# 72 instead of 48 tiles of an expert up-projection in the stage beside the choice of the experts, their results held in 48 places used in turn

## The chip, the core and the metric

One core of one Trainium2 chip runs the whole program. The metric is the device time of one execution in microseconds; the median of several executions is compared. The engines are named as in the profile: PE (matrix products, PEld its weight loads), DVE (vector), ACT (activations), POOL and SP (both used here mainly to issue transfers).

## The reference, cut to what matters

The model is two blocks over 256 tokens of width 2048. The change lies in the last layer of the second block, a mixture of 16384 tiny experts, each one row of `u_tab` and one row of `v_tab`:

```python
def peer(h, w_q, sub_keys, u_tab, v_tab):
    q = (h @ w_q).reshape(bsz, length, 8 heads, 2, 64)
    s = einsum("blhsk,hsnk->blhsn", q, sub_keys)        # scores against 2 x 128 keys
    s1, i1 = top_k(s[..., 0, :], 16); s2, i2 = top_k(s[..., 1, :], 16)
    cand_s = s1[..., :, None] + s2[..., None, :]         # 256 pairs per head
    top_s, pos = top_k(cand_s, 16)                       # 16 experts per head and token
    idx, g = take_along_axis(cand_i, pos), softmax(top_s)
    act = gelu(einsum("td,tkd->tk", x, u_tab[idx]))
    return einsum("tk,tkd->td", g * act, v_tab[idx])
```

## The kernel before, in words

The kernel does not gather rows. It computes gelu(x u) for all 16384 experts, multiplies by a gate that is zero where an expert was not chosen, and multiplies with all of `v_tab`. The 16384 experts are 128 tiles of 128; one tile is 128 experts by 256 tokens. The tensor `gates` holds 128 places of 256 columns.

All linear layers run through `linear_stage` (line 655). A tile's weights are four quarters of 512 columns. Each quarter goes through three engines: SP loads pairs of quarters into `ring` (`stream`), ACT rounds a quarter into `weights_hi` (`make_hi`, L200), DVE subtracts to get `weights_lo` (`make_lo`, L207), and PE multiplies both parts (L846, 32 matmuls a tile). `weights_hi` and `weights_lo` have four slots each, so one tile's quarters lie ready ahead of PE. After a tile ACT copies half of its sum out of PSUM (L760), DVE adds the other half (L816), and ACT applies gelu (L2456). All engines work in the order in which their instructions are written; semaphores tie them together: `core.multiplied` (a quarter is used up), `core.rounded`, `core.split`, `core.moved`, `core.summed`, `core.shaped` (gelu is done).

The order of the stages around the change, in `second_block` (line 2404):

1. `experts_first`: the first 48 tiles (EARLY_TILES) of the up-projection. Beside it runs the choice of the experts, `ExpertChoice` (line 2136). Its scores are on PE before the first and after the first tile; the searches (MAX8, FIND_INDEX8 and MATCH_REPLACE8 over 32 rows of 128 columns and 16 rows of 256 columns, each search in two rounds) and 14 large steps over 2048 columns are on DVE. `after_split` is called behind each split of a quarter and runs as many steps of the generator `vector` as are due: the planned nanoseconds of all steps (COLUMNS, 112260) are spread evenly over the quarters from the 9th (FIRST = 8) up to `self.quarters` = 4 x (tiles - 6). What is left runs after the stage's last tile. The arrays of the choice lie in `gates` from place EARLY_TILES to 115, the keys and queries in the last 12.
2. Gelu of early tile n goes to place n of `gates`. `ExpertChoice.issue` on POOL stores four tiles at a time to DRAM (`saved`, L2164) and waits for all stores at the end.
3. `gates_stage` (line 2322) writes the gates of all 128 tiles over the whole of `gates`.
4. `experts`: the remaining up-projection tiles, each multiplied into its gate (L2474), and then 128 tiles of down-projection. Beside the up-projection, `Returned` (line 2298) loads the stored tiles in pairs into two slots of `acts_back` (L2313, on POOL) and multiplies each into its gate on DVE (L2319, in `after_tile`). They are spread evenly over all but the last four tiles of the layer.

A layer with something beside it is written out tile by tile on PE, ACT and DVE; others run in loops.

Of the kernel before, what the change touches and what calls it, by code (L numbers as in the profile page):

```python
# [58 lines left out]
PEER_HEADS = 8  # L59
KEYS = 128  # L60
TOPK = 16
EARLY_TILES = 48
TWO_PI = 6.283185
MAGIC = 12582912.0

# [348 lines left out]
class Beside:  # L414
# [4 lines left out]
    def issue(self, pool):  # L419
        pass  # L420
# [1532 lines left out]
def glu_stage(core, y, parts, next_w):  # L1953

    with core.nc.Block() as block:
        @block.scalar
        def _(act):
            act.activation(y, y, ACT.Gelu_apprx_tanh)

    def gate(dve, n, slots):  # L1960
        dve.tensor_tensor(y[:, n, :], y[:, n, :], slots[0], ALU.mult)

    linear_stage(core, "glu", [
        Layer("w_glu", HT, [parts], shape=lambda act, n, slots: act.activation(slots[0], slots[0], ACT.Sigmoid),
              finish=gate, quarters=2, source=y)], next_w)
# [170 lines left out]
class ExpertChoice(Beside):  # L2136
# [23 lines left out]

    def issue(self, pool):
        for g in range(self.tiles // 4):
            pool.wait_ge(self.core.shaped, self.shaped + 4 * g + 4)
            pool.dma_start(self.saved[g], self.acts[:, 4 * g:4 * g + 4, :]).then_inc(self.done["saved"], 16)  # L2164
        pool.wait_ge(self.done["saved"], 16 * (self.tiles // 4))

    def scores(self, pe, t):
        for a in range(2):
# [225 lines left out]
def onto_stream(core, last=True):  # L2394

    def finish(dve, n, slots):
        ins = dve.tensor_tensor(core.x[:, n, :], core.x[:, n, :], slots[0], ALU.add)
        if last:
            core.dve.step(dve, ins)
            add_squares(core, dve, n, slots[0])  # L2400
    return finish


def second_block(core, out):


    nc = core.nc

    class S5:
        pass  # L2410

    with ExitStack() as mixers:
        sb = lambda name, shape, dt=F32: mixers.enter_context(nc.sbuf_tensor(name, shape, dt))
        proj, conv = sb("proj", [P, 3 * HT, T]), sb("conv", [P, HT, T])
        scans = ExitStack()
        sb2 = lambda name, shape: scans.enter_context(nc.sbuf_tensor(name, shape, F32))
        s5 = S5()
        s5.b, s5.c, s5.r = sb2("s5_b", [P, HT, 2, 2, 64]), sb2("s5_cc", [P, 3, PAIRS, 32]), sb2("s5_r", [P, PAIRS])
        with ExitStack() as projections:
            sb3 = lambda name, shape, dt=F32: projections.enter_context(nc.sbuf_tensor(name, shape, dt))  # L2420
            parts, h = sb3("in2_parts", [P, KD, 2, T], F32R), sb3("h_in2", [P, KD, T])
            rows = lambda part: (lambda n: proj[:, n + part * HT, :])
            linear_stage(core, "in2", [
                Layer("w_in_2", HT, [parts], into=rows(0), source=h, norm=Norm(core.x, core.prm["norm_mix"])),
                Layer("w_in_2", HT, [parts], first=2 * HT,
                      shape=lambda act, n, slots: act.activation(slots[0], slots[0], ACT.Sigmoid),
                      finish=lambda dve, n, slots: dve.tensor_copy(proj[:, n + HT, :], slots[0])),
                Layer("w_in_2", HT, [parts], first=4 * HT, into=rows(2)),
            ], ("w_glu", 0), beside=MixerSetup(core, s5, sb3))
        with scans:  # L2430
            local_mixers_stage(core, s5, proj, conv)
        y = proj[:, 2 * HT:, :]
        with nc.sbuf_tensor("glu_parts", [P, HT, 2, T], F32R) as parts:
            glu_stage(core, y, parts, ("w_out_2", 0))
        mem_parts = sb("mem_parts", [P, KD, 2, T], F32R)
        with ExitStack() as out2:
            sb2 = lambda name, shape, dt=F32: out2.enter_context(nc.sbuf_tensor(name, shape, dt))
            parts, h = sb2("out2_parts", [P, KD, 2, T], F32R), sb2("h_out2", [P, KD, T])
            mem, mem_squares = sb2("mem", [P, KD, T]), sb2("mem_squares", [P, KD, T])
            mem_sum, mem_std = sb2("mem_sum", [P, 1, T]), sb2("mem_std", [P, T])  # L2440
            group_norm_stage(core, conv[:], y, h)
            linear_stage(core, "mix2_out", [Layer("w_out_2", KD, [parts], finish=onto_stream(core), source=h, squares=True, steps=3)],
                         ("w_k", 0), loads=[(mem[:], "mem")], squares_of=(mem_squares[:], mem_sum[:]),
                         beside=NormBeside(core, mem, mem_sum[:, 0, :], core.prm["mem_norm"], mem_std[:], mem,
                                           mem_parts, at=5, squared=core.loaded_squared))
        q, k, v = proj[:, 0:KD, :], sb("k", [P, KD, T]), sb("v", [P, TT, 4, BANK])
        parts, h, std = sb("att_parts", [P, KD, 2, T], F32R), sb("h_att", [P, KD, T]), sb("att_std", [P, T])
        linear_stage(core, "mem_k", [Layer("w_k", KD, [mem_parts], into=lambda n: k[:, n, :])], ("w_q", 0),
                     beside=NormBeside(core, core.x, core.squares, core.prm["norm_mem"], std[:], h, parts))
        linear_stage(core, "mem_q", [Layer("w_q", KD, [parts], into=lambda n: q[:, n, :])], ("w_v", 0))  # L2450
        values_stage(core, mem_parts, v, ("w_o", 0))
        attention_stage(core, q, k, v, parts, h)
        linear_stage(core, "mem_out", [Layer("w_o", KD, [parts], finish=onto_stream(core), squares=True, steps=3)], ("w_peer_q", 0))
    with nc.sbuf_tensor("expert_parts", [P, KD, 2, T], F32R) as parts, nc.sbuf_tensor("gates", [P, KEYS, T], F32) as gates:
        saved = nc.dram_tensor("saved_acts", (EARLY_TILES // 4, P, 4, T), F32, kind="Internal").ap()
        gelu = lambda act, out, slots: act.activation(out, slots[0], ACT.Gelu_apprx_tanh)  # L2456
        with nc.sbuf_tensor("turned", [P, 3, T], F32) as turned:
            q = gates[:, KEYS - 8:KEYS, :]
            keys = gates[:, KEYS - 12:KEYS - 8, :].rearrange("p a (h n) -> p (a h) n", n=KEYS)
            linear_stage(core, "peer_q", [Layer("w_peer_q", PEER_HEADS, [parts], into=lambda n: q[:, n, :],  # L2460
                                                source=gates[:, 0:KD, :],
                                                norm=Norm(core.x, core.prm["norm_ffn"], squares=core.squares))],
                         ("w_u", 0), loads=[(keys, "peer_keys")])
            choice = ExpertChoice(core, q, keys, turned, gates[:, EARLY_TILES:KEYS - 12, :], gates[:, 0:EARLY_TILES, :], saved,
                                  EARLY_TILES, 6)
            linear_stage(core, "experts_first", [
                Layer("w_u", EARLY_TILES, [parts], shape=lambda act, n, slots: gelu(act, gates[:, n, :], slots)),
            ], ("w_u", 2 * EARLY_TILES), begin_next=False, beside=choice)
            gates_stage(core, turned, gates)
        with nc.sbuf_tensor("acts_back", [P, 4, T], F32) as back:  # L2470

            def gate_experts(dve, n, slots):
                at = n + EARLY_TILES
                dve.tensor_tensor(gates[:, at, :], gates[:, at, :], slots[0], ALU.mult)  # L2474

            up = Layer("w_u", KEYS - EARLY_TILES, [parts], finish=gate_experts, first=2 * EARLY_TILES,
                       shape=lambda act, n, slots: gelu(act, slots[0], slots))
            chunks = KEYS // KD
            down = [Layer("w_v_tab", KD, [parts], finish=onto_stream(core, c == chunks - 1), first=c * 2 * KD,
                          source=gates[:, c * KD:(c + 1) * KD, :], squares=c == chunks - 1,  # L2480
                          steps=3 if c == chunks - 1 else 0) for c in range(chunks)]
            linear_stage(core, "experts", [up, *down], None,
                         beside=Returned(core, back, saved, gates, EARLY_TILES, KEYS - EARLY_TILES - 4))
    rms_stage(core, "norm_last", core.x, core.x, KD, core.prm["final2"], squares=core.squares, store=out)
# [33 lines left out]
def two_block_kernel(nc, dram, out):  # L2518
    with ExitStack() as ctx:
        core = Core(nc, ctx, dram)  # L2520
        first_block(core)
        second_block(core, out)
# [127 lines left out]
```

## Time and profile before

| | us |
|---|---|
| median of 3 runs | 4280.64 (4276.46 to 4289.01) |
| profiled execution | 4285.37 |
| its span, first to last instruction | 4283.6 |
| PE busy / DVE busy / ACT busy | 3877.2 / 2815.2 / 2064.3 |
| stage beside the choice, 2nd to 47th gelu | 282.63 |
| up-projection after it, 2nd to 79th gelu | 427.87 |

The page gives each engine's busy time as a share of the span; a high share says that an engine is nearly always at work, and not in which stage it is late. The trace can be asked for stretches of time, for waits and for single instructions; times in it count from the span's start.

### The profile page before, as it was taken

How to read it: one execution, taken by the hardware profiler on the slowest of the kernel's cores; microseconds unless marked ns; L12 is line 12 of the kernel's file. 1: busy time of each engine (PE TensorE's matmuls, PEld its weight loads, DVE VectorE, ACT ScalarE, POOL GpSimd, SP SyncE). 2: the span in 40 equal slices, each digit the busy share in tenths (PEclk: the TensorE clock that was granted, in tenths of full speed). 3: DMA queues.
4: the chain of work that ended last, by engine and by line, in shares of the span. 5: the costliest groups of instructions: out<-in, count | busy, mean ns of one | idle time of the engine just before them, and what ended most of it. 6: DMA issues, size and time to landing. Idle time of an engine off the chain costs nothing. (4 is left out here: it accounts for less than half of the span.)

```text
span 4283.6 us, 66352 instructions
## 1 busy us (share of the span) xinstructions
PE 3877.2 (91%) x22156; PEld 3171.7 (74%) x22156; DVE 2815.2 (66%) x5280; ACT 2064.3 (48%) x3828; POOL 203.6 (5%) x242
## 2 busy tenths in 40 slices
PE   6699968778999999887699998998799999999998
PEld 0467744567888888774588877877688888888887
DVE  0553435777888667679686557687966666666667
ACT  0442330235666555455455434444955555555554
POOL 3011100000000000103100000000000000000000
PEclk9899979988999999998899999999999999999999
DMA  9686720034766666441255535555066665666665
GB/s 340 230 302 248 264 92 0 1 106 152 214 214 211 190 188 189 153 150 60 99 177 185 180 110 167 168 184 184 5 200 205 203 203 186 188 189 187 190 189 159
DMA packets 199380, 735.10 MB, mean 172 GB/s; under 512 B 22903, under 2 KB 22936, under 8 KB 197400
## 3 DMA queue, kind: packets, MB, share of 16 engines
q1 hardware_dynamic: 173992, 639.97, 47.6%
q0 software_dynamic: 25200, 92.64, 5.9%
q8 instruction: 116, 1.90, 0.2%
q14 instruction: 72, 0.59, 0.1%
HBM read 715.74 MB, written 16.78 MB: 171 GB/s over the span
## 5 line engine op out<-in xcount | busy, mean ns | idle before, releaser
L207 DVE TENSOR_TENSOR weights_lo<-ring,weights_hi 128x512 fp32r<-128x512 f32 x2240 | 1528.0, 695 | 978.1 <-ACT weights_hi L200 962.5
L200 ACT ACTIVATE weights_hi<-ring 128x512 fp32r<-128x512 f32 x2240 | 1396.4, 630 | 1373.9 <-PE ps L846 1308.4
L846 PE MATMUL ps<-expert_parts,weights_hi 128*128 128x512 f32 x4224 | 1466.9, 395 | 34.3 <-DVE weights_lo L207 26.8
L846 PE MATMUL ps<-expert_parts,weights_lo 128*128 128x256 f32 x4224 | 1142.6, 281 | 0.0
L846 PEld LDWEIGHTS ps<-expert_parts,weights_hi 128*128 128x128 f32 x4224 | 780.7, 189 | 205.2 <-issue 36.4
L846 PEld LDWEIGHTS ps<-expert_parts,weights_lo 128*128 128x128 f32 x4224 | 797.7, 189 | 20.4
L846 PE MATMUL ps<-mlp_parts,weights_hi 128*128 128x512 f32 x1024 | 354.0, 394 | 16.7 <-PEq L604 15.8
L846 PE MATMUL ps<-hidden,weights_hi 128*128 128x512 f32 x1024 | 351.5, 392 | 0.6 <-DVE weights_lo L207 0.6
L846 PE MATMUL ps<-mlp_parts,weights_lo 128*128 128x256 f32 x1024 | 277.4, 281 | 0.0
L846 PE MATMUL ps<-h_parts,weights_hi 128*128 128x512 f32 x704 | 266.1, 406 | 11.8 <-DVE weights_lo L207 11.8
L846 PE MATMUL ps<-hidden,weights_lo 128*128 128x256 f32 x1024 | 276.3, 280 | 0.0
L846 PEld LDWEIGHTS ps<-mlp_parts,weights_hi 128*128 128x128 f32 x1024 | 189.1, 189 | 55.5 <-issue 17.7
L846 PEld LDWEIGHTS ps<-hidden,weights_hi 128*128 128x128 f32 x1024 | 187.8, 188 | 38.4 <-DVE weights_lo L207 0.9
L846 PEld LDWEIGHTS ps<-mlp_parts,weights_lo 128*128 128x128 f32 x1024 | 193.8, 189 | 5.3
L377 PE MATMUL ps<-ada_ring,silu_c 128*32 128x512 f32 x768 | 148.9, 625 | 53.0 <-DMA ada_ring<-in_w_ada 52.9
L846 PEld LDWEIGHTS ps<-hidden,weights_lo 128*128 128x128 f32 x1024 | 192.5, 188 | 5.4
L846 PE MATMUL ps<-h_parts,weights_lo 128*128 128x256 f32 x704 | 193.2, 283 | 0.0
L846 PEld LDWEIGHTS ps<-h_parts,weights_hi 128*128 128x128 f32 x704 | 133.3, 190 | 75.1 <-issue 45.0
L846 PE MATMUL ps<-att_parts,weights_hi 128*128 128x512 f32 x512 | 176.1, 393 | 3.9 <-PEq L677 2.4
L846 PE MATMUL ps<-in_parts,weights_hi 128*128 128x512 f32 x384 | 136.7, 401 | 15.8 <-DVE weights_lo L207 8.5
L846 PEld LDWEIGHTS ps<-h_parts,weights_lo 128*128 128x128 f32 x704 | 133.5, 190 | 8.8
L846 PE MATMUL ps<-att_parts,weights_lo 128*128 128x256 f32 x512 | 138.1, 280 | 0.0
(460 smaller groups left out, 4972.7 us busy)
## 6 DMA issues: line engine op xcount, KB each, us to landing
ring<-in_w_mlp SPq DMA_DIRECT2D x256, 512.0 KB, 3.7
ring<-in_w_u SPq DMA_DIRECT2D x256, 512.0 KB, 4.1
ring<-in_w_v_tab SPq DMA_DIRECT2D x256, 512.0 KB, 3.7
ada_ring<-in_w_ada POOLq DMA_DIRECT2D x124, 512.0 KB, 6.5
ring<-in_w_mix SPq DMA_DIRECT2D x88, 512.0 KB, 5.6
ada_ring<-in_w_ada SPq DMA_DIRECT2D x68, 512.0 KB, 5.2
ring<-in_w_out SPq DMA_DIRECT2D x64, 512.0 KB, 3.7
ring<-in_w_in SPq DMA_DIRECT2D x48, 512.0 KB, 4.0
```

What stands on the lines that cost most here:

```text
L200: act.activation(core.hi[:, g % SLOTS], core.ring[:, slot, at:at + QUARTER], ACT.Copy).then_inc(core.rounded, 1)
L207: dve.tensor_tensor(core.lo[:, g % SLOTS], core.ring[:, slot, at:at + QUARTER], core.hi[:, g % SLOTS].bitcast(F32), ALU.subtract).then_inc ...
L377: mm = pe.matmul(self.core.ps[32 * j:32 * j + 32, self.bank(part), :], self.cond[:, k, :], self.ring[:, slot, (j % 2) * BANK:(j % 2 + 1) * ...
L846: mm = pe.matmul(out, part[:, g % SLOTS, k, :], moving, start=at == 0 and part is core.hi, stop=last and part is core.hi)
```

## The change

The number of early tiles and the number of places that hold their results become two constants. 72 tiles run beside the choice; tile n goes to place n mod 48. Before gelu of a tile from the 49th on, ACT waits until the store of the group that had this place has landed. POOL now waits after each store for it to land, so that the counter tells which stores are done. The arrays of the choice stay in places 48 to 115. The planned steps of the choice are spread over 4 x 66 - 8 = 256 quarters where it was 4 x 42 - 8 = 160. The later layer has 56 tiles where it had 80, and `Returned` brings back 72 tiles beside 52 of them where it brought 48 beside 76.

```diff
-EARLY_TILES = 48
+EARLY_TILES, EARLY_SLOTS = 72, 48
...
     def issue(self, pool):
         for g in range(self.tiles // 4):
+            at = 4 * g % EARLY_SLOTS
             pool.wait_ge(self.core.shaped, self.shaped + 4 * g + 4)
-            pool.dma_start(self.saved[g], self.acts[:, 4 * g:4 * g + 4, :]).then_inc(self.done["saved"], 16)
-        pool.wait_ge(self.done["saved"], 16 * (self.tiles // 4))
+            pool.dma_start(self.saved[g], self.acts[:, at:at + 4, :]).then_inc(self.done["saved"], 16)
+            pool.wait_ge(self.done["saved"], 16 * (g + 1))
+
+    def act_slot(self, act, n):
+        if n >= EARLY_SLOTS:
+            act.wait_ge(self.done["saved"], 16 * ((n - EARLY_SLOTS) // 4 + 1))
+        return self.acts[:, n % EARLY_SLOTS, :]
...
-            choice = ExpertChoice(core, q, keys, turned, gates[:, EARLY_TILES:KEYS - 12, :], gates[:, 0:EARLY_TILES, :], saved,
+            choice = ExpertChoice(core, q, keys, turned, gates[:, EARLY_SLOTS:KEYS - 12, :], gates[:, 0:EARLY_SLOTS, :], saved,
                                   EARLY_TILES, 6)
             linear_stage(core, "experts_first", [
-                Layer("w_u", EARLY_TILES, [parts], shape=lambda act, n, slots: gelu(act, gates[:, n, :], slots)),
+                Layer("w_u", EARLY_TILES, [parts], shape=lambda act, n, slots: gelu(act, choice.act_slot(act, n), slots)),
```

## Rows read from the trace of the kernel before

**Rows 1.** The page: busy time by engine, and the costliest groups of ACT and DVE.
```profile
PE 3877.2 (91%) x22156; PEld 3171.7 (74%) x22156; DVE 2815.2 (66%) x5280; ACT 2064.3 (48%) x3828; POOL 203.6 (5%) x242
...
L207 DVE TENSOR_TENSOR weights_lo<-ring,weights_hi 128x512 fp32r<-128x512 f32 x2240 | 1528.0, 695 | 978.1 <-ACT weights_hi L200 962.5
L200 ACT ACTIVATE weights_hi<-ring 128x512 fp32r<-128x512 f32 x2240 | 1396.4, 630 | 1373.9 <-PE ps L846 1308.4
```

**Rows 2.** Two stretches: busy time of each engine, beside and after the choice.
```profile
core 0: us, PE busy (x) PEld busy (x) DVE busy (x) ACT busy (x) POOL busy (x), PEclk, DMA share, GB/s
2710.19:2992.82 282.63, 259.19 (x1439) 219.44 (x1438) 228.53 (x619) 127.95 (x270) 5.96 (x11) 1.00 0.59 188
3122.23:3550.10 427.87, 427.87 (x2465) 376.28 (x2465) 279.12 (x510) 239.59 (x463) 11.84 (x22) 1.00 0.66 203
```

**Rows 3.** Timeline of ACT (start, duration): gelu of four tiles.
```profile
2710.19 0.42 ACT L2456 ACTIVATE gates<-experts_first_sums 128x256 f32<-128x256 f32 x1 [1.21 <-DVE experts_first_sums L816]
...
2992.82 0.42 ACT L2456 ACTIVATE gates<-experts_first_sums 128x256 f32<-128x256 f32 x1 [0.82 <-DVE experts_first_sums L816]
...
3122.23 0.42 ACT L2456 ACTIVATE experts_sums<-experts_sums 128x256 f32<-128x256 f32 x1 [0.82 <-DVE experts_sums L816]
...
3550.10 0.42 ACT L2456 ACTIVATE experts_sums<-experts_sums 128x256 f32<-128x256 f32 x1 [0.82 <-DVE experts_sums L816]
```

**Rows 4.** Waits, 2710 to 2993 us: total, times, longest.
```profile
PE ps L846 <- DVE weights_lo L207: 23.4, 36, 1.3
```

**Rows 5.** Timeline of DVE over one tile beside the choice.
```profile
2716.93 0.69 DVE L207 TENSOR_TENSOR weights_lo<-ring,weights_hi 128x512 fp32r<-128x512 f32 x1 [1.01 <-ACT weights_hi L200]
2717.54 0.48 DVE L2238 MAX8 gates<-gates 128x8 f32<-128x128 f32 x2
2717.94 0.68 DVE L207 TENSOR_TENSOR weights_lo<-ring,weights_hi 128x512 fp32r<-128x512 f32 x1
...
2721.29 0.40 DVE L816 TENSOR_TENSOR experts_first_sums<-experts_first_sums,ps 128x256 f32<-128x256 f32 x1
2722.70 0.69 DVE L207 TENSOR_TENSOR weights_lo<-ring,weights_hi 128x512 fp32r<-128x512 f32 x1 [1.01 <-ACT weights_hi L200]
```

**Rows 6.** Timeline of DVE: searches of 128 and of 256 columns.
```profile
2724.44 0.09 DVE L2243 MATCH_VALUE_LOAD gates<-gates 128x8 f32 x1
...
2725.23 0.67 DVE L207 TENSOR_TENSOR weights_lo<-ring,weights_hi 128x512 fp32r<-128x512 f32 x1
...
2882.37 0.09 DVE L2243 MATCH_VALUE_LOAD gates<-gates 128x8 f32 x1
...
2883.17 0.67 DVE L207 TENSOR_TENSOR weights_lo<-ring,weights_hi 128x512 fp32r<-128x512 f32 x1
```

**Rows 7.** Timeline of DVE: one of the 14 large steps.
```profile
2902.47 2.29 DVE L2285 TENSOR_TENSOR gates<-gates 128x2048 f32<-128x2048 f32 x1
2904.79 1.29 DVE L207 TENSOR_TENSOR weights_lo<-ring,weights_hi 128x512 fp32r<-128x512 f32 x2
```

**Rows 8.** Timeline of DVE over one tile of the later stage.
```profile
3177.35 0.41 DVE L816 TENSOR_TENSOR experts_sums<-experts_sums,ps 128x256 f32<-128x256 f32 x1
3178.25 0.42 DVE L2474 TENSOR_TENSOR gates<-gates,experts_sums 128x256 f32<-128x256 f32 x1 [0.48 <-ACT experts_sums L2456]
3178.59 0.42 DVE L2319 TENSOR_TENSOR gates<-gates,acts_back 128x256 f32<-128x256 f32 x1
3178.93 1.29 DVE L207 TENSOR_TENSOR weights_lo<-ring,weights_hi 128x512 fp32r<-128x512 f32 x2
3180.97 0.69 DVE L207 TENSOR_TENSOR weights_lo<-ring,weights_hi 128x512 fp32r<-128x512 f32 x1 [0.76 <-ACT weights_hi L200]
```

**Rows 9.** DMA issues: KB each, median us from issue to landing.
```profile
saved_acts<-gates POOLq DMA_DIRECT2D x12, 512.0 KB, 3.8
acts_back<-saved_acts POOLq DMA_DIRECT2D x24, 256.0 KB, 3.9
...
context<-in_ctx POOLq DMA_DIRECT2D x1, 2048.0 KB, 17.2
```

## The prediction

> **What bounds the kernel now.** I read the page's totals first: PE is busy for 91% of the span, DVE for 66% [rows 1]. So the question is only where PE stands still, and whether the change touches such a place. The change touches the two stages of the expert up-projection, so I read the table of stretches for both [rows 2]. In the stage beside the choice (2710 to 2993 us) PE is busy 259.2 of 282.6 us; in the stage after it (3122 to 3550 us) it is busy all of the 427.9 us. Both have PE at a granted clock of 1.00, and both do the same matmuls per tile.
>
> The price of one tile comes from the starts of gelu, one per tile [rows 3]. In the later stage 77 intervals take 3550.10 - 3122.23 = 427.87 us, 5.557 us a tile: PE's own pace. In the stage beside the choice 45 intervals take 2992.82 - 2710.19 = 282.63 us, 6.281 us a tile. At PE's pace they would be 250.06 us. So 32.6 us are lost there. The list of waits says to whom: PE waited 23.4 us in 36 pieces for DVE's low parts of the weights [rows 4], about the 23.4 us by which PE's busy time falls short. The rest of the 32.6 is not waited for by a busy-time count (ends of matmuls are modelled), so I take the tile pace, not the busy time.
>
> DVE is busy only 228.5 of 282.6 us there [rows 2], 81%, and still it is the bound. The timeline of one tile shows why [rows 5]. After DVE's sum (L816, start 2721.29) the next split (L207) starts at 2722.70, 1.41 us later, of which 1.01 us is idle: ACT has to do gelu of this tile (0.42 us, [rows 3]) and then round the next quarter of weights (0.63 us, [rows 1]) before DVE has anything to split. Four splits then follow, each 0.60 us after the other's start (0.61 from 2716.93 to 2717.54). So a DVE that lags needs 1.41 + 4 x 0.60 = 3.81 us a tile beside the steps of the choice. Check: this tile holds ten MAX8, two in 0.40 us; 3.81 + 10 x 0.20 = 5.81 against 5.77 measured.
>
> How much is the choice? DVE's busy time less its linear work is 228.53 - 45 x (4 x 0.60 + 0.41) = 102.1 us, and some 7 MAX8 (1.4 us) come before that stretch: 103.5 us. The code deals it out over 4 x 42 - 8 = 160 quarters, 40 tiles: 2.59 us a tile, and 3.81 + 2.59 = 6.40 us. Over 40 tiles that is 0.84 too much each, 34 us, against the 32.6 found. The model holds.
>
> **The change part by part.**
>
> *The choice over 72 tiles.* The share per quarter falls from 112260/160 = 702 to 112260/256 = 439 of the code's planned nanoseconds. The same 103.5 us lie on 64 tiles, 1.62 us each: 3.81 + 1.62 = 5.43 us, below PE's 5.557. DVE no longer bounds on the average, and the 32.6 us go. This is the only gain.
>
> Average isn't all. Where the real step is dearer than planned, a phase could still be over PE's pace. Searches: a FIND_INDEX8 of 256 columns with its load costs 0.40 us (two from 2882.37 to 2883.17), planned 0.416; one of 128 columns 0.26 us (three from 2724.44 to 2725.23), planned 0.288 [rows 6]. At 1754 planned ns a tile these are 4.2 x 0.40 = 1.69 and 6.1 x 0.26 = 1.60 us: 5.50 and 5.41, below 5.557. The 14 large steps cost 2.32 us (2902.47 to 2904.79) [rows 7], planned 2.2, and come every fifth quarter: four tiles with one and one without take 5 x 3.81 + 4 x 2.32 = 28.3 us against 27.8 of PE. Over their 17 tiles that is 2 us too much. Does the buffer hide it? A slot of weights is used again three quarters (4.17 us) after PE has freed it, and rounding and splitting take 0.63 + 0.70 us [rows 1], so DVE may lag some 2.8 us before PE stops. Bounds: 0 (the lag never reaches 2.8), and no buffer at all, where each large step stalls its tile by 3.81 + 2.32 - 5.56 = 0.57 us, 14 of them 8 us, and each second tile of the 46 in the searches (five steps instead of four) by 0.26 us, 6 us: 14 us. I take 2 us, near the lower end, since a lag of 0.6 a tile is far below 2.8.
>
> *24 tiles move.* They leave the later stage and enter the first: 24 x 5.557 us out, 24 x 5.557 in, if both keep PE's pace. Zero. The written-out instruction streams cover 48 + 80 = 128 tiles before and 72 + 56 after.
>
> *Their return.* 24 more products on DVE, now 72 beside 52 tiles, one or two a tile. In a tile with one, DVE goes from the sum (3177.35) to the product with the gate (3178.25), to the returned product (3178.59), to the split (3178.93), and has 0.76 us idle later [rows 8]. Its loop is 1.58 + 4 x 0.60 = 3.98 us, with two returned products 0.34 more, 4.32 us. Both fit in 5.557. PE hides it. If that cover were gone, it would be 24 x 0.34 = 8 us. Each product waits on DVE for a load from DRAM; behind it stand all splits. Loads take 3.9 us from issue to landing [rows 9]. One is issued when its slot is free, three products ahead of its first use, at least two tiles or 11.1 us. 7 us of slack: zero.
>
> *Stores.* Six more on POOL, and POOL now waits for each to land: 3.8 us [rows 9] in a period of four tiles, 22 us. Zero. Behind these waits only the next store is queued. The last store of the stage is issued and awaited as before. ACT gets 24 waits before its gelu for tiles 48 to 71; each is for a store some 44 tiles, 240 us, old. Not shown in the trace: between 0 and the 0.05 us from the sum's end (3177.35 + 0.41) to gelu's start, 3177.80 by the same spacing, that a due wait costs, 24 times, 1 us, off PE's path while DVE keeps up. I take 0. DMA carries 3.1 MB more each way; its share of the later stage, 0.66 [rows 2], would rise to about 0.72, with no wait of PE on DMA now: zero.
>
> Scores, the tail of the choice, the gates stage and the down-projection stay as they are.
>
> **Sum.** Profiled execution 4285.4 (span 4283.6 and 1.8 around it) - 32.6 + 2 = 4254.8 us. The median of the runs shown is 4.7 us lower, 4280.6; on that scale 4250 us.
>
> **The rivals.**
>
> *A, no buffer.* The steps' lumps reach PE: 14 us stay. 4285.4 - 32.6 + 14 - 4.7 = 4262 us. For it: tiles with one large step took 6.1 us and more; against it: those tiles were already lagging.
>
> *B, DVE still bounds, nearly no gain.* Reckon DVE by whole durations instead of starts: 0.41 + 1.01 + 4 x 0.69 + the choice. MAX8 pairs shown as 0.48 us instead of 0.40 make the choice 103.5 x 1.2 = 124 us, 1.94 a tile: 6.12 us. 64 tiles x 0.56 = 36 us would stay, no gain: 4281 us. Against it: split follows split at 0.60 us though it lasts 0.69, and the same reckoning for the tile of rows 5 gives 4.18 + 2.4 = 6.6 us, where 5.77 were measured. The Trainium skill (VectorE: DVE Perf Modes, section "The DRAIN you can't avoid") has the rule that speaks for B: the next vector operation does not start before the pipe of the one before is empty. By that rule the sum would be B's 4281 us instead of 4250; this case's trace, with its 0.60 against 0.69, disagrees.
>
> *C, slower: the loads of the returned tiles.* 36 pairs now come back within 52 tiles, one pair in 8.0 us, through two slots. A slot's turn is the load plus the 4 us between the two uses of a pair, so the period of a pair is (L + 4)/2 once L passes 12 us. At L = 13.8 it is 8.9 us and the 34 later pairs eat the gain; from there the kernel is slower. At 17.2 us, the slowest load of that queue shown (of 2 MB, [rows 9]), the period is 10.6 us: 34 x 2.6 = 88 us, 4250 + 88 = 4338 us. For it: the DMAs of that queue run beside 200 GB/s of weights; against it: they do so now, and take 3.9 us.
>
> **How the numbers follow.** Forecast 0.77, A 0.12, B 0.07, C 0.04. A measurement of this kernel can tell about 0.3%, 13 us, from no change: faster means below 4268. Forecast and A are faster: 0.89. B is the same: 0.07. C is slower: 0.04. The range starts at the forecast without the 2 us and with 6 us for the scatter of runs (4276 to 4289 shown): 4242. It ends past A with as much scatter: 4267.
>
> **What would show it.** In the stretch beside the choice gelu starts should be 5.56 us apart from start to end, PE's waits for L207 near zero, DVE's 1.01 us idle after the sum split into shorter ones behind each split. The stage should last about 72 x 5.557 + 13 us. The later stage should keep 5.56 us a tile with one and two L2319 beside it. A large-step phase with intervals of 6.1 us means A; intervals near 6.1 us throughout mean B; DVE waits for acts_back mean C. I am wrong if the two stages together save less than 18 us.

## The result, and the profile after

The changed kernel takes 4250.5 us (median, 4248.0 to 4262.6), the kernel before 4282.0 us in the same comparison: ratio 0.9930 (0.9916 to 0.9944), 31.4 us by the medians. The forecast was 4250 us. That the medians meet to within 1 us is luck: the four runs of the changed kernel spread over 14.6 us.

The page of the profile first. It hardly moved from [rows 1]; PE is busy for 91% of the span in both kernels:

```profile
PE 3872.2 (91%) x22156; PEld 3171.5 (74%) x22156; DVE 2807.8 (66%) x5280; ACT 2067.4 (49%) x3828; POOL 213.5 (5%) x260
```

Next the stages that were touched: from the second to the next to last gelu beside the choice, as in [rows 2], and from the first to the 54th gelu after it (columns as there).

```profile
2717.92:3103.97 386.05, 384.40 (x2207) 336.63 (x2206) 300.98 (x742) 206.38 (x414) 9.14 (x17) 1.00 0.67 211
3227.15:3521.66 294.51, 294.51 (x1697) 258.88 (x1697) 201.69 (x390) 164.88 (x319) 18.28 (x34) 1.00 0.73 220
```

PE is now busy 384.4 of 386.1 us beside the choice. The timeline of ACT gives the pace:

```profile
2717.92 0.42 ACT L2462 ACTIVATE gates<-experts_first_sums 128x256 f32<-128x256 f32 x1 [1.20 <-DVE experts_first_sums L816]
...
3103.97 0.42 ACT L2462 ACTIVATE gates<-experts_first_sums 128x256 f32<-128x256 f32 x1 [0.82 <-DVE experts_first_sums L816]
...
3227.15 0.42 ACT L2462 ACTIVATE experts_sums<-experts_sums 128x256 f32<-128x256 f32 x1 [0.82 <-DVE experts_sums L816]
...
3521.66 0.42 ACT L2462 ACTIVATE experts_sums<-experts_sums 128x256 f32<-128x256 f32 x1 [0.82 <-DVE experts_sums L816]
```

69 intervals take 386.05 us, 5.595 us a tile against 6.281 before [rows 3]. At 5.557 they would take 383.4, so 2.6 us are lost where 32.6 were. The later stage has 294.51/53 = 5.557 us a tile, as before. The waits of the first stretch (total, times, longest):

```profile
DVE weights_lo L207 <- ACT weights_hi L200: 82.4, 96, 1.0
ACT weights_hi L200 <- PE ps L846: 79.9, 119, 0.8
...
PE ps L846 <- DVE weights_lo L207: 1.6, 4, 0.5
```

PE waited 1.6 us for DVE, where it had waited 23.4 [rows 4]. ACT, in turn, waited 79.9 us for PE to free a slot of weights; before it was 13.0 us. One tile of DVE early in the choice, to be held against [rows 5]:

```profile
2718.89 0.69 DVE L207 TENSOR_TENSOR weights_lo<-ring,weights_hi 128x512 fp32r<-128x512 f32 x1 [1.00 <-ACT weights_hi L200]
2719.49 0.29 DVE L2244 MAX8 gates<-gates 128x8 f32<-128x128 f32 x1
2719.70 0.68 DVE L207 TENSOR_TENSOR weights_lo<-ring,weights_hi 128x512 fp32r<-128x512 f32 x1
2720.29 0.48 DVE L2244 MAX8 gates<-gates 128x8 f32<-128x128 f32 x2
2720.71 0.69 DVE L207 TENSOR_TENSOR weights_lo<-ring,weights_hi 128x512 fp32r<-128x512 f32 x1
2721.32 0.28 DVE L2244 MAX8 gates<-gates 128x8 f32<-128x128 f32 x1
2722.03 0.69 DVE L207 TENSOR_TENSOR weights_lo<-ring,weights_hi 128x512 fp32r<-128x512 f32 x1 [0.43 <-ACT weights_hi L200]
2722.64 0.48 DVE L2244 MAX8 gates<-gates 128x8 f32<-128x128 f32 x2
2723.04 0.40 DVE L816 TENSOR_TENSOR experts_first_sums<-experts_first_sums,ps 128x256 f32<-128x256 f32 x1
2724.45 0.69 DVE L207 TENSOR_TENSOR weights_lo<-ring,weights_hi 128x512 fp32r<-128x512 f32 x1 [1.01 <-ACT weights_hi L200]
```

Six MAX8 stand where ten stood. The 1.01 us behind the sum is still there, but before the fourth split DVE has a new idle stretch of 0.43 us: it has caught up with PE, and the chain waits for a slot. The prediction had said that the 1.01 us would split into shorter idle times behind each split; they stay, and shorter ones come beside them.

The profiled execution of the changed kernel is the slowest of its four, 4262.6 us (span 4260.7). Its extra time lies ahead of the change: the first score matmul (L2171 before, L2177 after) starts at 2692.65 us, before it started at 2684.90. So traces are best compared from there to the end of the span: 4283.6 - 2684.90 = 1598.7 us before, 4260.7 - 2692.65 = 1568.0 us after, 30.7 us less. The sum had said 32.6 - 2 = 30.6. Of the 30.7 us, 30.0 are the stage's own (32.6 - 2.6).

### The profile page after: what moved, and what is told of

Read it like the earlier page. It is cut to its first block and busy times, and to the rows that moved or that the text cites. A ratio compares the mean times of both kernels' runs of the same rounds, so it can differ in the third digit from the quotient of the medians.

```text
span 4260.7 us, 66415 instructions
## 1 busy us (share of the span) xinstructions
PE 3872.2 (91%) x22156; PEld 3171.5 (74%) x22156; DVE 2807.8 (66%) x5280; ACT 2067.4 (49%) x3828; POOL 213.5 (5%) x260
## 5 line engine op out<-in xcount | busy, mean ns | idle before, releaser
L846 PE MATMUL ps<-mlp_parts,weights_hi 128*128 128x512 f32 x1024 | 354.2, 394 | 16.7 <-PEq L604 15.8
```

The source lines that it names most:

```text
L846: mm = pe.matmul(out, part[:, g % SLOTS, k, :], moving, start=at == 0 and part is core.hi, stop=last and part is core.hi)
```

## The experiments

My theory: beside the choice DVE runs in a loop of 3.81 us a tile (sum, ACT's gelu and rounding, four splits) plus its share of the choice's 103.5 us. It binds while this is above PE's 5.557 us. The rivals: B (DVE is bound by its own instructions, counted in whole durations), C (the returned tiles), a gain from the small edits, and a gain that grows with each tile moved. In the table "from the scores" is the span's end less the start of the first score matmul in the run's trace. Each ratio is to the kernel before as it ran in the same comparison; its medians there were 4284.4 us (e1 to e4), 4280.0 us (e5 to e7) and 4285.9 us (e8 to e10).

| run | median us | ratio to before | from the scores, us | less than before |
|---|---|---|---|---|
| before | 4282.0 | | 1598.7 | |
| changed | 4250.5 | 0.9930 (0.9916 to 0.9944) | 1568.0 | 30.7 |
| e1_edits_48 | 4283.0 | 0.9997 (0.9988 to 1.0007) | 1598.7 | 0.0 |
| e2_tiles_60 | 4257.7 | 0.9936 (0.9919 to 0.9953) | 1579.8 | 18.9 |
| e3_late_gelu_48 | 4255.7 | 0.9933 (0.9916 to 0.9949) | 1569.0 | 29.7 |
| e4_late_gelu_72 | 4249.2 | 0.9915 (0.9896 to 0.9933) | 1564.5 | 34.2 |
| e5_tiles_96 | 4265.8 | 0.9962 (0.9950 to 0.9975) | 1582.0 | 16.7 |
| e6_back_26 | 4250.1 (one run) | | 1566.5 | 32.2 |
| e7_back_12 | 4302.0 (one run) | | 1611.4 | -12.7 |
| e8_places_96 | 4251.3 | 0.9925 (0.9909 to 0.9942) | 1565.7 | 33.0 |
| e9_after_again | 4253.5 | 0.9926 (0.9914 to 0.9938) | 1565.9 | 32.8 |
| e10_late_72_again | 4249.5 | 0.9914 (0.9901 to 0.9926) | 1564.6 | 34.1 |

The changed kernel and e9 are the same kernel; their 1568.0 and 1565.9 us show how far this count scatters from trace to trace, some 2 us. Most of it arises between the last gelu beside the choice and the first of the later stage: 117.64 us in the first trace, 115.29 in e9 (first row below: changed; second: e9). The instructions there are the same. At the start of the later stage the granted clock stood at 0.50 for some 7 us in the first trace and at 1.00 in e9 (third and fourth row: 16 matmuls against 29 in the same 6.7 us):

```profile
3109.51:3227.15 117.64, 86.95 (x561) 73.72 (x562) 104.48 (x332) 103.46 (x205) 1.62 (x3) 0.93 0.07 22
3100.47:3215.76 115.29, 83.83 (x561) 71.23 (x562) 104.50 (x332) 103.37 (x204) 1.62 (x3) 0.97 0.07 22
3215.60:3222.30 6.70, 5.08 (x16) 4.33 (x17) 3.46 (x6) 2.82 (x5) 1.08 (x2) 0.50 0.63 213
3206.50:3213.20 6.70, 5.00 (x29) 4.44 (x30) 4.16 (x7) 3.95 (x7) 1.09 (x2) 1.00 0.65 191
```

The traces of before, e1 and e2 have such a stretch too, e6, e7 and e9 have none, the others one of half the length. So up to 3 us of the last column can come from it, and the loss against PE's pace within a stage is the sharper count.

**The small edits alone.**

```diff
-EARLY_TILES, EARLY_SLOTS = 72, 48
+EARLY_TILES, EARLY_SLOTS = 48, 48
```

> The changed kernel with 48 early tiles: POOL waits after each store and the other edits stay, the number of tiles is that of before. Theory (DVE's loop of 3.81 us a tile plus the choice's share is the bound, only the spreading over more tiles helps): same as before, ratio 1.000, 6.28 us a tile beside the choice. Rival (POOL's waits after each store, or another of the small edits, gives part of the gain): faster than before by up to 30 us.

Measured: 0.9997. Its 45 intervals lost 32.5 us, before it was 32.6. POOL's waits after each store neither cost nor gain. ACT's new wait does not occur with 48 tiles, so this run says nothing of it.

**60 early tiles** (EARLY_TILES = 60).

> 60 early tiles. Theory: the choice's 103.5 us lie on 52 tiles, 1.99 us each; 3.81 + 1.99 = 5.80 us a tile, 0.24 above PE's 5.557, so 52 x 0.24 = 13 us stay lost of 32.6: about 20 us faster than before, ratio 0.9954, and some 5.8 us between gelu starts while the choice runs. Rival (each moved tile brings the same, 30 us / 24 = 1.25 us): 12 tiles bring 15 us, ratio 0.9965.

The medians give 26.7 us, with an interval of about 20 to 35: the theory's 20 lies at its edge, the rival's 15 outside. The trace settles it better. From the second to the next to last gelu there are 57 intervals:

```profile
2703.66 0.42 ACT L2462 ACTIVATE gates<-experts_first_sums 128x256 f32<-128x256 f32 x1 [1.21 <-DVE experts_first_sums L816]
...
3034.24 0.42 ACT L2462 ACTIVATE gates<-experts_first_sums 128x256 f32<-128x256 f32 x1 [0.82 <-DVE experts_first_sums L816]
```

They take 330.58 us, 13.8 us above 57 x 5.557 (the theory said 13). The count from the scores gives 18.9 us less than before. Half of the added tiles brings some 60% of the gain (18.9 of 30.7): the curve bends as a loop does that comes down to PE's pace.

**Gelu behind the next rounding, 48 tiles.** EARLY_TILES is 48. ACT's order alone is changed: gelu of a tile is put aside and runs behind the next quarter that ACT rounds. DVE has the same work at the same places.

```diff
+        layer.late = isinstance(beside, ExpertChoice)
...
+                if make is make_hi and layer.late:
+                    def make_layer(core, act, g, i, per, base):
+                        make_hi(core, act, g, i, per, base)
+                        while waiting:
+                            waiting.pop(0)()
...
                     if layer.shape is not None:
-                        act.wait_ge(core.summed, i * layer.unroll + (layer.N + s + 3))
-                        layer.shape(act, n, slots(layer, n, s)).then_inc(core.shaped, 1)
+                        def late():
+                            act.wait_ge(core.summed, i * layer.unroll + (layer.N + s + 3))
+                            layer.shape(act, n, slots(layer, n, s)).then_inc(core.shaped, 1)
+                        if layer.late and n < layer.tiles - 1:
+                            waiting.append(late)
+                        else:
+                            while waiting:
+                                waiting.pop(0)()
+                            late()
```

> 48 early tiles, but ACT rounds the first quarter of the next weights before it does gelu of the tile. DVE has the same work. Theory (the 1.01 us in which DVE waits for ACT's gelu and rounding is part of the loop): the wait falls to about 0.25 us (rounding 0.63 us begins with DVE's sum of 0.41 us), the loop to 3.05 us, with the choice 2.59 it is 5.64 us a tile; some 3 us and lumps of the large steps stay, 3 to 10 us in all: 23 to 29 us faster than before, ratio 0.993 to 0.995. Rival B (DVE is bound by its own work alone, counted in whole durations, 6 us and more a tile): no change, ratio 1.000.

Measured: 0.9933; 29.7 us less from the scores, 0.7 us above the 23 to 29 us expected, which is less than the scatter. The 44 intervals from the second gelu on lost 3.4 us. The timeline of DVE in this run, a tile with ten MAX8 as in [rows 5]:

```profile
2764.55 0.40 DVE L829 TENSOR_TENSOR experts_first_sums<-experts_first_sums,ps 128x256 f32<-128x256 f32 x1
2764.87 0.69 DVE L207 TENSOR_TENSOR weights_lo<-ring,weights_hi 128x512 fp32r<-128x512 f32 x1
2765.47 0.48 DVE L2257 MAX8 gates<-gates 128x8 f32<-128x128 f32 x2
2766.13 0.69 DVE L207 TENSOR_TENSOR weights_lo<-ring,weights_hi 128x512 fp32r<-128x512 f32 x1 [0.18 <-ACT weights_hi L200]
```

The split follows the sum at once and the 1.01 us is gone. The waits of 0.2 us elsewhere are PE's pace: ACT, for which DVE waits there, itself waited 78.8 us for PE in this stretch, where it had been 13.0. So nearly the whole gain can be had without moving a tile. This rules out rival B: with the same DVE instructions the loss fell from 32.6 to 3.4 us. And it says what had been the bound: a chain from DVE over ACT and back, and not DVE's work by itself.

**Both together.**

> 72 early tiles and gelu behind the next rounding. Theory: the loop is 3.05 + 1.62 = 4.67 us, 0.9 us below PE's pace, and even a tile with a large step needs 3.05 + 2.32 = 5.37 us, so nothing of the 2.6 us is left: 5.557 us between gelu starts throughout, ratio to before 0.992, to the changed kernel not distinguishable. Rival (the 2.6 us come from where the large steps stand among the quarters): they stay.

PE waited for DVE not once between 2710 and 3088 us in this trace; the 68 intervals from the second gelu on lost nothing (-0.4 us). The rival (the lumps stay) falls. I had said 5.557 us between gelu starts throughout; that was wrong in form, since gelu itself is late (up to 7.4 us apart) behind the large steps, without PE noticing. From the scores it is 34.2 us less than before.

**96 early tiles** (EARLY_TILES = 96).

> 96 early tiles, 96 returned beside 28. Theory: beside the choice 3.81 + 103.5/88 = 4.99 us, below PE's 5.557, with large steps every seventh quarter; 0 to 1 us stays lost in that stage, some 2 us less than with 72. More moved tiles bring nothing else: ratio to before about 0.992 if the returns stay hidden. Rival C (the loads of the returned tiles bind): three or four products stand behind one another in a tile, DVE's loop is 3.64 + 3.43 x 0.34 = 4.8 us plus a wait for the load of up to 1 us: up to 7 us lost over 28 tiles, ratio 0.994. Rival (the gain grows with the tiles moved, 1.25 us each): 60 us, ratio 0.986.

Measured: 0.9962, so 16.3 us by the ratio and 16.7 from the scores, half of what I expected. The stage beside the choice did nearly as the theory says (93 intervals lost 1.5 us, 0 to 1 expected). The loss is in the later stage: 30 intervals of gelu from 3356.96 us take 182.95 us, 16.2 above PE's pace, where I had allowed 7. The waits from 3356.96 to 3534.36 us show rival C at work:

```profile
DVE gates L2325 <- DMA acts_back<-saved_acts: 17.2, 10, 3.4
```

One such wait in DVE's timeline, the issue of its load on POOL, and PE's and ACT's timelines around it:

```profile
3463.97 1.11 DVE L2325 TENSOR_TENSOR gates<-gates,acts_back 128x256 f32<-128x256 f32 x3
3468.52 0.42 DVE L2325 TENSOR_TENSOR gates<-gates,acts_back 128x256 f32<-128x256 f32 x1 [3.44 <-DMA acts_back<-saved_acts]
3468.86 2.49 DVE L207 TENSOR_TENSOR weights_lo<-ring,weights_hi 128x512 fp32r<-128x512 f32 x4
```
```profile
3464.69 1.21 POOL L2319 DMA_DIRECT2D acts_back<-saved_acts  x2 [4.46 <-DVE gates L2325]
```
```profile
3469.69 0.47 PE L846 MATMUL ps<-expert_parts,weights_hi 128*128 128x512 f32 x1 [2.72 <-DVE weights_lo L207]
...
3471.16 0.63 PE L846 MATMUL ps<-expert_parts,weights_hi 128*128 128x512 f32 x1
```
```profile
3463.17 0.42 ACT L2462 ACTIVATE experts_sums<-experts_sums 128x256 f32<-128x256 f32 x1 [0.82 <-DVE experts_sums L816]
...
3471.71 0.42 ACT L2462 ACTIVATE experts_sums<-experts_sums 128x256 f32<-128x256 f32 x1 [3.81 <-DVE experts_sums L816]
...
3478.82 0.42 ACT L2462 ACTIVATE experts_sums<-experts_sums 128x256 f32<-128x256 f32 x1 [0.82 <-DVE experts_sums L816]
```

A slot holds a pair and is loaded again only when both tiles are used. The products beside one tile form a batch, of three or four here. Where a batch of four starts with the second tile of a pair, its last tile belongs to the pair after the next, whose load starts only when the batch's first product has freed the slot. Here that product starts at 3463.97, the load at 3464.69, and it lands at 3468.5: DVE waits nearly a whole load (3.7 us in the median). Four of the batches meet the pairs in this way. I had counted an average; the pairs make it a matter of how batches and pairs meet.

**The returns packed closer, 72 tiles.** The last argument of `Returned`, 52 in the changed kernel, becomes 26 and 12.

> The changed kernel with its 72 tiles returned beside 26 up tiles instead of 52: 2.8 products a tile. Theory: DVE's loop is 3.64 + 2.8 x 0.34 = 4.6 us, a pair is due every 4.0 us, and its load (4.5 us with 2 slots) allows one about every 3.3 us: gelu starts stay 5.56 us apart. Rival C: they widen.

> 72 tiles returned beside 12 up tiles, six products a tile with two slots of two: the third pair of each tile can be loaded only after the first is used, so DVE waits about 3.8 us a tile; its loop is 3.64 + 6 x 0.34 + 3.8 = 9.5 us against 5.557, 12 tiles lose about 47 us, less 3 us for the weights laid ready. That is rival C made true: a wait for acts_back on DVE and gelu starts 9 to 10 us apart. If loads did not hold DVE, they would stay 5.7 us apart.

e6: 5.56 us a tile but for one of 6.32 us; DVE waited for loads twice, 2.2 us in all. As expected. e7: the first 13 intervals are 8.4 to 9.5 us long. Its one run takes 51.9 us more than that of e6. From the scores it is 44.9 us more than e6 and 43.4 more than the changed kernel (1611.4 against 1566.5 and 1568.0), where 44 were expected. The wait is the one named:

```profile
DVE gates L2325 <- DMA acts_back<-saved_acts: 40.3, 12, 3.8
...
PE ps L846 <- DVE weights_lo L207: 29.4, 12, 3.7
```

The granted clock was 0.87 in the mean over these 13 intervals (its column is the third from the end), for which the 44 us had no term; how much of the 43.4 us is the clock's isn't separated:

```profile
3221.02:3338.80 117.78, 88.42 (x417) 74.25 (x417) 66.80 (x150) 40.98 (x79) 18.29 (x34) 0.87 0.58 192
```

So rival C is real, and the change lies well clear of it at 1.4 products a tile.

**96 tiles, five places of one tile.** `acts_back` has five places of one tile instead of two of a pair, and a load brings one tile.

```diff
-        for m in range(0, self.tiles, 2):
-            slot = m // 2 % 2
-            if m >= 4:
-                pool.wait_ge(self.used, m - 2)
-            pool.dma_start(self.back[:, 2 * slot:2 * slot + 2, :], self.saved[m // 4, :, m % 4:m % 4 + 2, :]).then_inc(
-                self.landed[slot], 16)
+        for m in range(self.tiles):
+            if m >= 5:
+                pool.wait_ge(self.used, m - 4)
+            pool.dma_start(self.back[:, m % 5, :], self.saved[m // 4, :, m % 4, :]).then_inc(self.landed[m % 5], 16)
...
-            dve.wait_ge(self.landed[m // 2 % 2], 16 * (m // 4 + 1))
+            dve.wait_ge(self.landed[m % 5], 16 * (m // 5 + 1))
```

> 96 early tiles, returned one by one into five places instead of in pairs into two slots; three or four products a tile as in the run with 96 tiles and pairs, which lost 16 us there against PE's pace. Theory: a place is free as soon as its one tile is used, four of five lie ready at each batch, and the next four have 5.56 - 1.4 = 4.2 us and the fifth place to land: DVE waits little, 0 to 4 us stay of the 16 and no wait of 3 us. Ratio to before 0.992 to 0.993. Rival (the 16 us are the cost of more products on DVE, or of DMA traffic, whatever the slots): the 16 us stay, ratio 0.996.

Measured: 0.9925; gelu starts in the later stage:

```profile
3338.14 0.42 ACT L2460 ACTIVATE experts_sums<-experts_sums 128x256 f32<-128x256 f32 x1 [0.82 <-DVE experts_sums L816]
...
3504.84 0.42 ACT L2460 ACTIVATE experts_sums<-experts_sums 128x256 f32<-128x256 f32 x1 [0.82 <-DVE experts_sums L816]
```

30 intervals, 166.70 us, 5.557 each: all of the 16 us is back, with as many products and as much traffic. The slots were the cause. The run changes two things of them, one tile a load and room for a fifth tile, and no run tells which of the two does it. And 96 tiles bring no more than 72 (0.9925 against 0.9930 and 0.9926): the gain doesn't grow with the tiles once the loop is below PE's pace.

**The two best, side by side.**

> The changed kernel again, on the same chip as the next, to compare the two: ratio to before 0.993.

> 72 early tiles and gelu behind the next rounding, beside the changed kernel on the same chip. Theory: 2.6 us (0.06%) less than it, from the stage beside the choice; the medians lie 0 to 5 us apart. Rival: no difference at all, since the lag was hidden.

0.9926 (0.9914 to 0.9938) and 0.9914 (0.9901 to 0.9926); the medians are 4.0 us apart, the intervals overlap. The times lean to a gain from the late gelu without settling it. From the scores it is 1.3 us less than e9 and 3.4 less than the first trace; expected were 2.6. The stage beside the choice tells it apart: the changed kernel loses 2.6 and 2.7 us there in its two traces and PE waits 1.6 us for DVE in each, with the late gelu it loses nothing (-0.4 us) in e4 and in e10 and PE does not wait at all. The count from the scores hides 1.5 us of this: e10 has a stretch of the lower clock between the stages and e9 has none (116.81 us there against 115.29).

## Why the prediction was right

- *Where the time was lost.* 32.6 us by the pace of gelu, not the 23.4 us of waits. What the change gave back in the stage, 30.0 us, is more than the waits: the pace was the right count.
- *The loop.* 3.81 us plus the choice's share. At 40, 52, 64 and 88 tiles for the choice the loss was 32.6, 13.8, 2.6 and 1.5 us; the loop alone says 34, 13, 0 and 0. Shown by e2, e5 and, from the other side, e3.
- *The lumps.* I took 2 us from 0 to 14; the lost time was 2.6 us, and e4 shows that it is DVE's lag: with a shorter loop it vanishes. Of PE's 1.6 us of waits 1.3 lie at the large steps (2980 to 3072 us), where the prediction put them. Its reason for a value near the lower end was wrong, though, and that the size came out is partly luck: the lag is not 0.6 us but adds up over the four tiles in a row that have a large step. The prediction also has it that intervals of 6.1 us in the large steps mean rival A. They came, and A was not so. Gelu in the large steps of the changed kernel:

```profile
3019.89 0.42 ACT L2462 ACTIVATE gates<-experts_first_sums 128x256 f32<-128x256 f32 x1 [1.06 <-DVE experts_first_sums L816]
...
3026.04 0.42 ACT L2462 ACTIVATE gates<-experts_first_sums 128x256 f32<-128x256 f32 x1 [1.44 <-DVE experts_first_sums L816]
...
3044.52 0.42 ACT L2462 ACTIVATE gates<-experts_first_sums 128x256 f32<-128x256 f32 x1 [3.23 <-DVE experts_first_sums L816]
...
3048.35 0.42 ACT L2462 ACTIVATE gates<-experts_first_sums 128x256 f32<-128x256 f32 x1 [1.06 <-DVE experts_first_sums L816]
```

  Gelu follows DVE: 6.16 us a tile over four tiles (3019.89 to 3044.52), 2.4 us behind PE's pace in all, and 3.83 in the fifth tile, without a large step. The buffer takes up nearly all of it, and PE's waits are what tells A.
- *The moved tiles, the stores, the wait of ACT.* Zero each. The 5.557 us of the later stage show it for the moved tiles, e1 for the stores. ACT's wait is due in tiles 49 to 72: in the changed kernel's trace gelu starts 0.03 us after the end of the sum in tiles 49 to 71, as in tiles 2 to 48, and e4 has all 24 waits and loses nothing.
- *The returns.* Zero at 72 tiles beside 52, though a load took 4.5 us where it had been 3.9, and DMA's share rose to 0.73 (0.72 was said). Rival C's price was put as an average period of (L + 4)/2, with a turning point at a load of 13.8 us. e5 shows that this formula is too kind for closer packing: loads of 3.7 us were enough to lose 16 us, because of the way in which batches and pairs meet. For the changed kernel itself this didn't matter.
- *Rival B.* Shown wrong by e3. The prediction gives it the rule of the Trainium skill (VectorE: DVE Perf Modes, "The DRAIN you can't avoid") that the next vector operation starts only when the pipe of the one before is empty, and calls the trace in disagreement. It left out that the same section adds an exception: "A next op that is not held starts earlier". The traces agree with the exception: a split of 0.69 us is followed by MAX8 0.60 us after its start, two MAX8 take 0.40 us where each lasts 0.28. So the page did not speak for B here.

## What to carry to other kernels

An engine that is busy for only 81% of a stage can be what bounds it, if its idle time is a wait that recurs in a loop over another engine: take the loop's length from starts in the timeline, and compare it with the pace of the busiest engine in a stage where that one never waits. Such a loop can be eased by giving it less per turn (spreading the side work, as here) or by taking a link out of it (ACT's order), and the second needs no moved work. Side work gives nothing more once the loop is below the pace, and what brings the moved tiles back has to be checked by batch and slot, not by its mean rate.

## What the runs showed of the hardware that I had not expected

A stall of PE can cost more than the stall. In e5 PE stood idle for 2.72 us at 3467 us; the stretches just before, from 0.9 us behind its new start, and after:

```profile
3460.00:3466.50 6.50, 6.50 (x40) 5.70 (x39) 3.87 (x9) 3.75 (x7) 1.32 (x3) 1.00 0.79 250
3470.60:3473.70 3.10, 3.10 (x11) 2.62 (x11) 2.62 (x8) 1.01 (x2) 0.49 (x1) 0.50 0.73 201
3474.00:3480.00 6.00, 6.00 (x36) 5.28 (x35) 3.33 (x8) 3.23 (x7) 0.42 (x1) 1.00 0.70 244
```

The granted clock was 0.50, the lower of its two levels (1.2 GHz), for some 3 us; a matmul of 512 columns took 0.63 us where it takes 0.39, and the tile of that stretch 7.11 us where it takes 5.56. So 2.98 us of stall (8.54 us between gelu starts) were followed by another 1.55 us. It does not follow each time. The other three long stalls of that stage were 2.54, 2.43 and 2.85 us; behind the first two the clock stayed at 1.00, behind the third it fell:

```profile
3386.50:3390.00 3.50, 3.50 (x21) 3.07 (x21) 3.02 (x8) 1.58 (x3) 0.20 (x1) 1.00 0.56 154
3428.00:3431.00 3.00, 3.00 (x18) 2.62 (x18) 2.52 (x7) 1.05 (x3) 0.00 (x0) 1.00 0.38 127
3514.80:3518.10 3.30, 3.30 (x12) 2.82 (x11) 2.82 (x8) 1.05 (x2) 0.45 (x1) 0.50 0.67 196
```

So some 3.1 of the 16.2 us that this stage lost came with the lower clock (intervals of 7.11 and 7.10 us behind the two stalls), and the rest with the waits. The 3.0 us for which PE stands idle ahead of the later stage are a like case: in the first trace of the changed kernel the clock fell with them, in e9 it did not (the rows beneath the table). The shorter stalls of before, at most 1.3 us [rows 4], left the clock at 1.00 [rows 2].

The other: most of the scatter of this kernel comes from the part ahead of the change. The scores started between 2672.7 and 2692.7 us in these traces, while from there to the end two traces of one kernel differ by 2 us. For a change late in a program the count from a fixed instruction told more than the medians did. Why the first part scatters stays open.
